# Second stack, layer 0: the context's norm and queries computed beside the end of the first stack

## The chip, the cores and the metric

The kernel runs on one core of one Trainium2 chip. The time is that of the device for one execution, in microseconds (us); the median of the runs counts.

## The reference

Two transformer stacks run one behind the other on x, 256 tokens of width 1024, all in float32.

The first stack has two layers. Each adds four branches to x, every one normed before and after: a gated feed-forward block (ffn0), a mixer, a second feed-forward block (ffn1) and a gated per-layer embedding (ple): `x = x + rmsnorm(sigmoid(h @ w_ple_gate) * (p @ w_ple_proj))`.

The second stack takes x and a context of another 256 tokens, which the first stack doesn't touch. Its layer 0 begins so:

```python
h  = modulate(rmsnorm(x,  norm1_g), sh1,  sc1)     # 256 tokens
hc = modulate(rmsnorm(xc, norm1_g), shc1, scc1)    # 256 context tokens
q, k, v    = split(h  @ w_qkv)                     # 1024 columns each; q and k are rotated by position
qc, kc, vc = split(hc @ w_qkv)                     # the context is not rotated
```

Attention over both, an output projection, a router and a mixture of 32 experts follow, then layer 1 of the same kind and a final norm. Shifts and scales (modulation) come from another input, by products with mod_w that are made piecewise beside the first stack.

## The kernel before

Each of the five engines has one program, a fixed list of instructions in order; an engine that waits holds back all that stands behind in its list. `pe_program`, `act_program`, `dve_program`, `pool_program` and `sp_program` write these lists for TensorE, ScalarE, VectorE, GpSimd and the queue that issues the loads. Semaphores carry the dependences: `s["name"].up(...)` is the signal, `s["name"].at(...)` the wait.

x and the context lie side by side in `k.x` (128 partitions, 8 tiles of the width, 512 columns: 256 tokens of x, then 256 of the context). `S` is 256, `KT` is 8, `D` is 1024. PSUM has 8 banks (`k.ps`) of 512 columns.

The end of the first stack (`pe_ple` and its companions, layer 1): the gate's quarters 0 and 1 are multiplied (L1281), the embedding projected (L1298), then quarters 2 and 3 (L1271), whose weights are the last loads of the stack (L1245). ScalarE makes the sigmoids (L1318), VectorE multiplies them with the projection (L1335). The post norm is a chain over four engines: squares (ScalarE L470), pair sums (VectorE L488, L491), the sum over partitions by a product with ones (TensorE L481), root (ScalarE L472), reciprocal (VectorE L493), and for each of the 8 tiles scale and add into x (VectorE L497, L500). The last of these is `added (1, "ple", 7)`.

The start of the second stack waits for that last add. Then ScalarE squares all 512 columns of each tile (L1376), TensorE sums them (L1369), ScalarE takes two roots (L1385), VectorE two reciprocals (L1403) and 16 scaled tiles (L1408), and ScalarE adds the shifts (L1390): 256 columns at a time, x and context in turn. SP issues the constants (L2973) and the six chunks of w_qkv, 2 MB each, into `slots2` (L1354), behind the same add.

`pe_project("q0")` makes 8 query tiles of 512 columns (x and context in one product, L1443), each followed by the rotation of the tile before it (L1425), for which ScalarE copies the x half (L1463); ScalarE also copies the context half (L1465), and VectorE finishes the rotation (L1477, L1479, L1482). `pe_project("k0")` does the same for the keys, `pe_values` makes the values (L1497), then comes attention. The experts' weights are issued at L1902, each behind a tile of TensorE that frees its slot.

A float32 product is recorded as two MATMUL and two LDWEIGHTS records.

Of the kernel before, what the change touches and what calls it, by code (L numbers as in the profile page):

```python
# [13 lines left out]
P = 128  # L14
D = 1024
# [18 lines left out]
class Signal:  # L34
# [27 lines left out]
    "pe_mod": "mod_product mod_turned", "pe_mixer": "mx_product mx_pe", "pe_ple": "ple_product ple_p_turned", "pe_tokens": "t_summed",  # L62
# [4 lines left out]
    "act_mixer": "mx_act", "act_ple": "ple_gated", "act_tokens": "t_squared t_root t_made", "act_project": "pr_copied", "act_values": "v_out_act",  # L67
# [9 lines left out]
    "pool_setup": "zeros_set upad_zero", "pool_squares": "squares conv_u", "pool_moe": "pool_ended", "pool_pairs": "xs_paired",  # L77
# [81 lines left out]
class Kernel:  # L159
# [99 lines left out]
    def second_memory(self):  # L259
        self.top = self.keep_top  # L260
        self.slots2 = [self.take(4096) for _ in range(6)]
        self.const2 = self.constants("constants_const2", second_constants(), 1850)
        self.h2 = self.take(KT, 2 * S)
        self.Q, self.K, self.V = (self.take(KT, 2 * S) for _ in range(3))
        self.pad = self.arena[:, self.top:self.top + 4096]
        self.sqb = self.take(4, BANK)
        self.take(KT * S - 4 * BANK)
# [9 lines left out]
        self.Kflat = self.K.rearrange("p a b -> p (a b)")  # L277
        self.vtok = [self.Vflat.rearrange("p (t d) -> p t d", t=4), self.Vflat[:, 0:1024].rearrange("p (t d) -> p t d", t=4)]
# [185 lines left out]
def act_post_norm(k, l, name, y, ready):  # L464

    act, s = k.nc.scalar, k.s
    act.activation(k.spare, k.eps, ACT.Sqrt)
    for b in range(4):
        act.wait_ge(*ready[b])
        act.activation(k.sq[:, 2 * b:2 * b + 2, :], y[:, 2 * b:2 * b + 2, :], ACT.Square).then_inc(*s["post_squared"].up(l, name, b))  # L470
    act.wait_ge(*s["post_summed"].at(l, name))
    act.activation(k.rscale[:, 0:S], k.ps[:, 0, 0:S], ACT.Sqrt, scale=1.0 / D, bias=k.eps[:, 0:1]).then_inc(*s["post_root"].up(l, name))  # L472
# [173 lines left out]
def pe_ffn(k, l, f):  # L646
# [61 lines left out]
    for c in range(2, CHUNKS):  # L708
        m = mods_of(l, f, c)
        gate_up(2 * c, k.h)  # L710
        down(2 * c - 1)
        gate_up(2 * c + 1, k.h)
        if m is not None:
            pe_modulate(k, l, m, m % 2, (2 * c + 2) % 4)
        down(2 * c)
        if m is not None:
            pe_modulation_out(k, l, m, (2 * c + 3) % 4, k.mrow, 0)
    down(2 * CHUNKS - 1)
# [30 lines left out]
def act_ffn(k, l, f):  # L749
# [25 lines left out]
    act_post_norm(k, l, f"ffn{f}", k.banks(4, 4, S), ends)  # L775

# [461 lines left out]
def sp_ple(k, l):  # L1238
# [17 lines left out]
    if l == 0:  # L1256
        sp_modulation(k, l, 10)
        sp_modulation(k, l, 11)
    sp.wait_ge(*s["ple_product"].at(l, "up", 3))
    quarter(3)  # L1260


def pe_ple(k, l):
# [40 lines left out]
    quarter(3, k.h)  # L1304
    pe_post_norm(k, l, "ple")


def act_ple(k, l):
    act, s = k.nc.scalar, k.s
    for b in range(4):  # L1310
        e = k.e[:, 2 * b:2 * b + 2, :]
        if b < 2:
            act.wait_ge(*s["ple_scaled"].at(l, b))
            src = e
        else:
            act.wait_ge(*s["ple_product"].at(l, "gate", b))
            src = k.banks(b, 1, S)
        act.activation(e, src, ACT.Sigmoid).then_inc(*s["ple_gated"].up(l, b))  # L1318
    act_post_norm(k, l, "ple", k.e, [s["ple_done"].at(l, b) for b in range(4)])


def dve_ple(k, l):
# [42 lines left out]
def pe_sums(k, tag, t, w):  # L1365

    pe, s = k.nc.tensor, k.s
    pe.wait_ge(*s["t_squared"].at(tag, t))
    pe.matmul(k.ps[:, 7, 0:w], k.c["ones"], k.sqb[:, t % 4, 0:w], start=(t == 0), stop=(t == KT - 1), skip_group_check=True).then_inc(*s["t_summed"].up(tag, t))  # L1369


def act_square(k, tag, t, w):
    act, s = k.nc.scalar, k.s
    if t >= 4:
        act.wait_ge(*s["t_summed"].at(tag, t - 4))
    act.activation(k.sqb[:, t % 4, 0:w], k.x[:, t, 0:w], ACT.Square).then_inc(*s["t_squared"].up(tag, t))  # L1376
# [37 lines left out]
def pe_project(k, tag, first, slots, ntok, tiles, dup=False, made=None, behind=None):  # L1414


    pe, s = k.nc.tensor, k.s
# [10 lines left out]
    for j in range(tiles):  # L1428
        slot = slots[j // 4]
        w = chunk_view(k, slot, n)  # L1430
        if j % 4 == 0:
            pe.wait_ge(*s[f"slot{slot}"].at("chunk", first + j // 4))
# [1529 lines left out]
def sp_program(k, ms, out):  # L2962
# [9 lines left out]
    sp.wait_ge(*s["zeroed"].at(1, D // 2))  # L2972
    sp.dma_start(*k.const2).then_inc(*s["const2"].up())  # L2973
    a = k.a
    w = a["a_w_qkv_2"][0]
    for n in range(6):
# [23 lines left out]
def pe_program(k, ms):  # L3000
    pe, s = k.nc.tensor, k.s
    pe_setup(k)
    for l in range(DEPTH):
# [33 lines left out]
def act_program(k, ms):  # L3037
# [39 lines left out]
def dve_program(k, ms):  # L3077
# [8 lines left out]
    V.wait_ge(*s["zeroed"].at(1, D // 2))  # L3086
    dve_modulated(k, "a0", 0, 0, (0, 1))
    V.wait_ge(*s["const2"].at())
    dve_project(k, "q0", k.Q, 2 * S, 8)
# [18 lines left out]
def pool_program(k, ms):  # L3108
# [3 lines left out]
    for l in range(DEPTH):  # L3112
# [3 lines left out]
        pool_prepare(k, l, "ffn1", added_before(k, l, "mix"))  # L3116
        pool_prepare(k, l, "ple", added_before(k, l, "ffn1"))
# [39 lines left out]
```

## Time and profile before

| | |
|---|---|
| median of 3 runs | 3017.91 us (3016.14 to 3020.22) |
| the profiled execution: its time, its span | 3016.83 us, 3015.6 us |
| busy: TensorE, VectorE, ScalarE, GpSimd | 2670.6, 751.3, 483.6, 212.8 us |
| last gate product of the ple block ends | 1396.58 us after the start |
| last add into x ends | 1413.25 us |
| first query product begins, first key product begins | 1429.08, 1489.76 us |

How to read the rows below. PE is TensorE's products, PEld its weight loads, DVE VectorE, ACT ScalarE, POOL GpSimd, SPq the load queue. L1443 is a line of the kernel. A row of the chain has the start, the length and what ran; the chain is followed back from the last instruction to whatever released it. A row of stretches has, for each engine in the order PE, PEld, DVE, ACT, POOL, the busy time and the instructions, then TensorE's granted clock (1.00 is 2.4 GHz, 0.50 is 1.2 GHz), the share of the DMA engines and GB/s. A row of a timeline has the start, the time from the first start to the last end of the merged instructions (for loads, of their issuing), the engine, line, operation, tiles and count, and in brackets the idle time before and what ended it. A row of groups has the count, then busy us, mean ns of one, idle us before them. A row of DMA issues has the count, the size and the us from issue to landing.

### The profile page before, as it was taken

What the parts mean: (1) busy time and instruction counts of PE and PEld (TensorE: products, weight loads), DVE (VectorE), ACT (ScalarE), POOL (GpSimd) and SP (SyncE); (2) the same over time, 40 slices, a digit from 0 to 9 for tenths busy, and PEclk for the clock granted to TensorE, in tenths of its full rate; (3) what the DMA queues carried; (4) which work ended last, traced back from release to release, by engine and by line L of the source; (5) the groups of instructions that cost most, each with busy time, mean ns of one, the idle gap of its engine ahead of it and who ended that gap; (6) DMA issues with size and microseconds to landing.
All of it is one profiled execution on the core that took longest, in us unless ns stands there. A gap on an engine that the chain in (4) does not pass through costs nothing.

```text
span 3015.6 us, 57462 instructions
## 1 busy us (share of the span) xinstructions
PE 2670.6 (89%) x24534; PEld 1982.5 (66%) x24534; DVE 751.3 (25%) x2039; ACT 483.6 (16%) x1182; POOL 212.8 (7%) x392
## 2 busy tenths in 40 slices
PE   8999999999999999997998899988776998776676
PEld 7888788887888778885444456665555466544444
DVE  2002520023002430014116621211113163332323
ACT  2001310011001220003104521110002151000001
POOL 1001010011001010001000012221211000000000
PEclk9999999999999999998999999999988999999999
DMA  7553465546453455542320039999996314999997
GB/s 265 179 171 112 157 239 173 174 157 223 153 192 111 162 202 203 195 157 106 144 84 29 3 144 375 411 411 421 420 420 236 105 52 179 420 419 419 419 419 296
DMA packets 251832, 690.23 MB, mean 229 GB/s; under 512 B 15247, under 2 KB 142942, under 8 KB 235230
## 3 DMA queue, kind: packets, MB, share of 16 engines
q1 hardware_dynamic: 240352, 675.27, 59.0%
q0 software_dynamic: 7552, 10.76, 1.0%
q8 instruction: 173, 2.83, 0.4%
q10 hardware_dynamic: 3710, 0.99, 0.1%
q14 instruction: 45, 0.37, 0.0%
HBM read 669.95 MB, written 17.04 MB: 228 GB/s over the span
## 4 chain that ended last, share of the span: by engine, by line
PE 76%; DMA 12%; DVE 5%; issue 3%; ACT 3%; SPq 0%; ACTq 0%; POOL 0%; POOLq 0%; DVEq 0%
PE ps L663 18%; DMA arena<-in_moe_w_up 11%; PE ps L674 10%; PE ps L1443 5%; PE ps L2287 5%; PE ps L2262 3%; PE ps L2790 3%; PE ps L2302 3%; PE ps L1497 2%; PE ps L894 2%; PE ps L687 2%; PE ps L1054 2%; PE ps L2042 2%; PE ps L2751 1%; PE ps L2814 1%
## 5 line engine op out<-in xcount | busy, mean ns | idle before, releaser
L663 PE MATMUL ps<-arena 128*128 128x256 f32 x2560 | 568.6, 379 | 3.5 <-DVE arena L745 3.5
L663 PEld LDWEIGHTS ps<-arena 128*128 128x128 f32 x2560 | 483.0, 189 | 73.8 <-issue 4.1
L674 PE MATMUL ps<-arena 128*128 128x256 f32 x1408 | 318.0, 379 | 0.0
L674 PEld LDWEIGHTS ps<-arena 128*128 128x128 f32 x1408 | 264.9, 189 | 46.1 <-issue 8.4
L2287 PE MATMUL ps<-arena 128*32 128x128 f32 x6016 | 193.6, 286 | 61.1 <-issue 58.6
L2287 PEld LDWEIGHTS ps<-arena 128*32 128x32 f32 x6016 | 177.6, 115 | 71.9 <-issue 67.6
L2790 PE MATMUL ps<-arena 128*32 128x128 f32 x4096 | 138.7, 294 | 82.3 <-issue 80.6
L787 DVE TENSOR_TENSOR arena<-arena,ps 128x256 f32<-128x256 f32 x76 | 32.1, 422 | 638.4 <-ACT arena L755 633.7
L2790 PEld LDWEIGHTS ps<-arena 128*32 128x32 f32 x4096 | 125.5, 118 | 90.0 <-issue 89.0
L1443 PE MATMUL ps<-arena 128*128 128x512 f32 (+1 forms) x384 | 162.6, 601 | 5.6 <-ACT arena L1390 5.6
L755 ACT ACTIVATE arena<-ps 128x256 f32<-128x256 f32 x76 | 29.2, 384 | 675.1 <-PE ps L663 675.1
L1443 PEld LDWEIGHTS ps<-arena 128*128 128x128 f32 (+1 forms) x384 | 64.6, 174 | 94.7 <-issue 91.7
L532 POOL TENSOR_TENSOR arena<-arena 128x256 f32<-128x256 f32 x64 | 42.8, 670 | 1081.3 <-DVE arena L500 1072.4
L2262 PE MATMUL ps<-arena 128*32 128x256 f32 x1536 | 103.1, 395 | 11.6 <-issue 8.5
L2369 POOL DMA_DIRECT2D expert_out<-arena x200 | 100.3, 502 | 69.8 <-issue 30.9
L2302 PE MATMUL ps<-arena 128*32 128x256 f32 x1504 | 94.3, 387 | 0.2
L2814 PE MATMUL ps<-arena 128*32 128x256 f32 x1024 | 62.1, 381 | 35.9 <-DVE arena L2902 35.9
L2347 DVE TENSOR_TENSOR arena<-arena,ps 128x128 f32<-128x128 f32 x47 | 13.5, 288 | 310.6 <-ACT arena L2317 310.6
L2262 PEld LDWEIGHTS ps<-arena 128*32 128x32 f32 x1536 | 57.4, 112 | 37.8 <-issue 14.0
L894 PE MATMUL ps<-arena 128*128 128x256 f32 x352 | 77.4, 379 | 0.0
L2751 PE MATMUL ps<-arena 128*32 128x256 f32 x528 | 69.8, 637 | 6.2 <-DVE arena L2006 3.3
L894 PEld LDWEIGHTS ps<-arena 128*128 128x128 f32 x352 | 66.3, 189 | 9.5
(457 smaller groups left out, 3091.6 us busy)
## 6 DMA issues: line engine op xcount, KB each, us to landing
arena<-in_moe_w_gate SPq DMA_DIRECT2D x64, 2048.0 KB, 24.8
arena<-in_moe_w_up SPq DMA_DIRECT2D x64, 2048.0 KB, 25.5
arena<-in_moe_w_down SPq DMA_DIRECT2D x64, 2048.0 KB, 30.4
arena<-in_mod_w SPq DMA_DIRECT2D x24, 2048.0 KB, 13.0
arena<-in_w_gate SPq DMA_DIRECT2D x44, 1024.0 KB, 5.3
arena<-in_w_up SPq DMA_DIRECT2D x44, 1024.0 KB, 7.9
arena<-in_w_down SPq DMA_DIRECT2D x44, 1024.0 KB, 4.8
arena<-in_w_in SPq DMA_DIRECT2D x12, 1024.0 KB, 6.0
```

The lines of the kernel that those rows point to most:

```text
L663: last = pe.matmul(k.ps[:, T % 4, off:off + S], w[:, t, T % 2 * P:(T % 2 + 1) * P], h[:, t, :], start=(t == 0), stop=(t == KT - 1), skip_g ...
L674: last = pe.matmul(acc[:, t, :], d[:, T % 2, t * P:(t + 1) * P], k.hid[:, T % 4, :], start=(T == 0 and t % 2 == 0), stop=end, skip_group_c ...
L687: last = pe.matmul(k.ps[:, T, off:off + S], w[:, t, T * P:(T + 1) * P], k.hu[:, t, :], start=(t == 0 and off == 0), stop=(t == KT - 1), sk ...
L894: last = pe.matmul(dst, w[:, t, j * P:(j + 1) * P], src[:, t, :], start=(t == 0), stop=(t == KT - 1), skip_group_check=True)
L1443: last = pe.matmul(k.ps[o:o + m, j % 4, 0:ntok], w[:, t, c0:c0 + m], k.h2[:, t, 0:ntok], start=(t == 0), stop=(t == KT - 1), tile_position ...
L2262: last = k.nc.tensor.matmul(k.ps[32 * q:32 * q + 32, 1, 0:256], m.pick[:, t, :], m.rows[:, t, 256 * q:256 * q + 256], start=(t == 0), stop ...
L2287: last = pe.matmul(ps[BL * q:BL * q + BL, 0, a:a + F], m.xeT[:, t, :], wv[:, t, F * q:F * q + F], start=(t == 0), stop=(t == KT - 1), tile ...
L2302: last = pe.matmul(ps[BL * q:BL * q + BL, 3, 0:W], m.hT[:, f, :], wd[:, f, W * q:W * q + W], start=(f == 0), stop=(f == 3), tile_position= ...
L2369: k.nc.gpsimd.dma_start(k.ybuf[bass.ds(b * BL, BL), W * q:W * q + W], m.yring[BL * q:BL * q + BL, bass.ds((b & 3) * W, W)]).then_inc(which ...
L2751: last = k.nc.tensor.matmul(k.ps[32 * q:32 * q + 32, bank, 0:256], m.pick[:, t, :], rows, start=(t == 0), stop=(t == 1), tile_position=(0, ...
L2790: last = pe.matmul(ps[BL * q:BL * q + BL, 0, a:a + F], m.xeT[:, t, :], wv[:, t, F * q:F * q + F], start=(t == 0), stop=(t == KT - 1), tile ...
L2814: last = pe.matmul(ps[BL * q:BL * q + BL, 3, 0:W], m.hT[:, f, :], wd[:, f, W * q:W * q + W], start=(f == 0), stop=(f == 3), tile_position= ...
```

## The change

Context and x are treated apart at the start of the second stack.

- GpSimd squares the context (8 tiles) and adds the squares up behind its ffn1 squares of layer 1, in the place of the later queries.
- TensorE sums them over partitions with one product ahead of the last down product of ffn1; ScalarE takes the root behind ffn1's post norm.
- VectorE's gain, reciprocal and 8 scaled context tiles stand in the ple block between the two `ple_scaled` and the gate multiplications; ScalarE's 8 shifts stand between the sigmoids 1 and 2.
- The query weights (two halves of 2 MB) go to the places of the keys and the values. Half 0 is issued once the modulation product 11 is done, half 1 right behind quarter 3 of the gate. The constants follow on quarter 2's product. Behind the last add SP issues only chunks 2 to 5.
- The context's 8 query tiles of 256 columns: 0 and 1 ahead of the ple block's post norm sums, 2 to 5 behind them, then the 8 sums of x, now over 256 columns, then tiles 6 and 7. ScalarE copies them to `k.Q` at the matching places.
- `pe_project("q0")` makes 8 tiles of 256 columns. x has its squares in 8 places of their own, so a square waits for no sum; each square waits for its own add instead of the last. The dummy root of L3053 goes.

```diff
 def act_post_norm(k, l, name, y, ready):
...
+    if (l, name) == (1, "ple"):
+        act_context_queries(k, (0, 1))
     act.wait_ge(*s["post_summed"].at(l, name))
...
 def pe_ffn(k, l, f):
...
+    if (l, f) == (1, 1):
+        pe_context_sum(k)
     down(2 * CHUNKS - 1)
     pe_post_norm(k, l, name)
...
 def act_ffn(k, l, f):
...
+    if (l, f) == (1, 1):
+        act_context_root(k)
...
 def sp_ple(k, l):
...
+    else:
+        sp.wait_ge(*s["mod_product"].at(l, 11))
+        sp_query_weights(k, 0)
     sp.wait_ge(*s["ple_product"].at(l, "up", 3))
     quarter(3)
+    if l == 1:
+        sp_query_weights(k, 1)
+        sp.wait_ge(*s["zeroed"].at(1, D // 2))
+        sp.wait_ge(*s["ple_product"].at(l, "gate", 2))
+        sp.dma_start(*k.const2).then_inc(*s["const2"].up())
...
+def sp_query_weights(k, i):
+    sp, s = k.nc.sync, k.s
+    sp.dma_start(k.qweights[i], columns(k.a["a_w_qkv_2"][0], 512 * i)).then_inc(*s[f"slot{i}"].up("chunk", i))
...
 def pe_ple(k, l):
...
     quarter(3, k.h)
+    if l == 1:
+        pe_context_queries(k, (0, 1))
     pe_post_norm(k, l, "ple")
...
 def act_ple(k, l):
...
         act.activation(e, src, ACT.Sigmoid).then_inc(*s["ple_gated"].up(l, b))
+        if (l, b) == (1, 1):
+            act_context_shifts(k)
...
 def dve_ple(k, l):
...
+    if l == 1:
+        dve_modulated(k, "a0", 0, 0, (1,))
     for b in range(4):
...
+CONTEXT_BANKS = (1, 2, 3, 4, 5, 6, 1, 2)
+
+def pool_context_squares(k):
+    pool, s = k.nc.gpsimd, k.s
+    pool.wait_ge(*s["added"].at(1, "mix", KT - 1))
+    for t in range(KT):
+        pool.tensor_tensor(k.csq[:, t, :], k.x[:, t, S:2 * S], k.x[:, t, S:2 * S], ALU.mult).then_inc(*s["c_squares"].up(t))
+        if t > 0:
+            pool.wait_ge(*s["c_squares"].last())
+            pool.tensor_tensor(k.csq[:, 0, :], k.csq[:, 0, :], k.csq[:, t, :], ALU.add).then_inc(*s["c_squares"].up(t, "added"))
+
+def pe_context_sum(k):
+    pe, s = k.nc.tensor, k.s
+    pe.wait_ge(*s["c_squares"].at(KT - 1, "added"))
+    pe.matmul(k.ps[:, 0, S:2 * S], k.c["ones"], k.csq[:, 0, :], start=True, stop=True, skip_group_check=True).then_inc(*s["c_summed"].up())
+
+def act_context_root(k):
+    act, s = k.nc.scalar, k.s
+    act.wait_ge(*s["zeroed"].at(1, D // 2))
+    act.wait_ge(*s["c_summed"].at())
+    act.activation(k.at[:, 0, S:2 * S], k.ps[:, 0, S:2 * S], ACT.Sqrt, scale=1.0 / D, bias=k.eps[:, 0:1]).then_inc(*s["t_root"].up("a0", 1))
+
+def act_context_shifts(k):
+    act, s = k.nc.scalar, k.s
+    for t in range(KT):
+        H = k.h2[:, t, S:2 * S]
+        act.wait_ge(*s["t_normed"].at("a0", t, 1))
+        act.activation(H, H, ACT.Identity, bias=k.mod_col(0, 0, t, 1)).then_inc(*s["t_made"].up("a0", t, 1))
+
+def pe_context_queries(k, tiles):
+    pe, s = k.nc.tensor, k.s
+    free = [s["ple_scaled"].at(1, 1), s["ple_gated"].at(1, 2), s["ple_gated"].at(1, 3), s["ple_done"].at(1, 0), s["ple_done"].at(1, 1), s["ple_done"].at(1, 2),
+            s["c_out"].at(0), s["c_out"].at(1)]
+    for j in tiles:
+        if j % 4 == 0:
+            pe.wait_ge(*s[f"slot{j // 4}"].at("chunk", j // 4))
+        if j == 0:
+            pe.wait_ge(*s["t_made"].at("a0", KT - 1, 1))
+        pe.wait_ge(*free[j])
+        for t in range(KT):
+            last = pe.matmul(k.ps[:, CONTEXT_BANKS[j], 0:S], k.qweights[j // 4][:, t, j % 4 * P:(j % 4 + 1) * P], k.h2[:, t, S:2 * S],
+                             start=(t == 0), stop=(t == KT - 1), skip_group_check=True)
+        last.then_inc(*s["c_tile"].up(j))
+
+def act_context_queries(k, tiles):
+    act, s = k.nc.scalar, k.s
+    for j in tiles:
+        act.wait_ge(*s["c_tile"].at(j))
+        act.activation(k.Q[:, j, S:2 * S], k.ps[:, CONTEXT_BANKS[j], 0:S], ACT.Copy).then_inc(*s["c_out"].up(j))
...
 def pe_project(k, tag, first, slots, ntok, tiles, dup=False, made=None, behind=None):
...
+        w = chunk_view(k, slots[j // 4], n) if slots else k.qweights[j // 4]
+        if not slots and j == 1:
+            pe.wait_ge(*s["c_out"].at(7))
...
 def pe_program(k, ms):
...
+    pe_context_queries(k, (2, 3, 4, 5))
     for t in range(KT):
-        pe_sums(k, "a0", t, 2 * S)
+        pe_sums(k, "a0", t)
+    pe_context_queries(k, (6, 7))
     pe.wait_ge(*s["const2"].at())
-    pe_project(k, "q0", 0, (0, 1), 2 * S, 8, made=[s["t_made"].at("a0", t, 1) for t in range(KT)])
+    pe_project(k, "q0", 0, None, S, 8, made=[s["t_made"].at("a0", t, 0) for t in range(KT)])
...
 def act_program(k, ms):
...
-    act.wait_ge(*s["added"].at(1, "ple", KT - 1))
-    act.wait_ge(*s["zeroed"].at(1, D // 2))
-    act.activation(k.lnA[:, 0, KT:KT + 1], k.eps, ACT.Sqrt)
     for t in range(KT):
-        act_square(k, "a0", t, 2 * S)
-    act_modulated(k, "a0", 0, 0, (0, 1))
-    act_project(k, "q0", k.Q, 2 * S, 8)
+        act.wait_ge(*s["added"].at(1, "ple", t))
+        act_square(k, "a0", t)
+    act_context_queries(k, (2, 3, 4, 5))
+    act_modulated(k, "a0", 0, 0, (0,))
+    act_context_queries(k, (6, 7))
+    act_project(k, "q0", k.Q, S, 8)
```

## Rows read from the trace of the kernel before

**Rows 1.** The page: the chain that ended last, by engine.

```profile
PE 76%; DMA 12%; DVE 5%; issue 3%; ACT 3%; SPq 0%; ACTq 0%; POOL 0%; POOLq 0%; DVEq 0%
```

**Rows 2.** Stretches from the last gate quarters to the end of the queries.

```profile
1382.70:1396.60 13.90, 13.87 (x64) 11.76 (x63) 0.69 (x1) 0.60 (x1) 0.00 (x0) 1.00 0.23 77
1396.60:1404.90 8.30, 3.50 (x8) 2.28 (x8) 2.08 (x3) 4.19 (x8) 0.00 (x0) 0.80 0.00 0
1404.90:1413.25 8.35, 0.00 (x0) 0.00 (x0) 7.79 (x17) 0.45 (x1) 0.00 (x0) 0.70 0.00 0
1413.25:1429.10 15.85, 9.47 (x17) 3.92 (x17) 5.20 (x9) 6.71 (x14) 0.00 (x0) 0.72 0.95 354
1429.10:1489.76 60.66, 60.62 (x145) 27.99 (x146) 12.98 (x34) 10.69 (x30) 0.00 (x0) 0.97 0.45 166
```

**Rows 3.** The chain that ended last, in order of time, 1099 to 1503.

```profile
1099.27 1.83 PE ps L481 x8
...
1382.70 13.88 PE ps L1271 x64
...
1401.33 3.51 PE ps L481 x8
...
1414.04 9.46 PE ps L1369 x16
...
1424.10 3.38 DVE arena L1403 x2
...
1429.08 15.63 PE ps L1443 x32
...
1452.02 0.43 PE ps L1425 x2
...
1489.06 0.70 PE ps L1425 x2
1489.76 13.76 PE ps L1443 x32
```

**Rows 4.** Groups of instructions, shapes apart, 1370 to 1489.8.

```profile
L1271 PEld LDWEIGHTS ps<-arena 128*128 128x128 f32 x64 | 12.1, 189 | 1.8
...
L1408 DVE SCALAR_TENSOR_TENSOR arena<-arena 128x256 f32<-128x256 f32 x16 | 6.4, 482 | 0.0
```

**Rows 5.** Timeline of the ple block: loads issued, ScalarE and VectorE.

```profile
1350.42 32.69 SPq L1245 DMA_DIRECT2D arena<-in_w_ple_gate  x2
...
1356.10 0.51 ACT L519 ACTIVATE arena<-arena 128x256 f32<-128x256 f32 x1 [3.07 <-DVE arena L500]
...
1376.45 1.28 DVE L1330 TENSOR_TENSOR arena<-ps,arena 128x512 f32<-128x512 f32 x2
...
1389.67 0.60 ACT L1318 ACTIVATE arena<-ps 128x512 f32<-128x512 f32 x1 [11.27 <-PE ps L1271]
```

**Rows 6.** VectorE's add beside GpSimd (min/median/max ns); timeline of ffn1's start.

```profile
L500 DVE TENSOR_TENSOR arena<-arena x8: 417/606/718, 1355.6 to 1361.5; 128x256 f32<-128x256 f32 x8
...
1114.43 1.53 POOL L535 TENSOR_TENSOR arena<-arena 128x256 f32<-128x256 f32 x2
...
1122.16 2.36 DVE L579 TENSOR_TENSOR arena<-arena 128x1024 f32<-128x1024 f32 x2
...
1125.56 0.43 DVE L787 TENSOR_TENSOR arena<-arena 128x256 f32<-128x256 f32 x1 [0.22 <-ACT arena L755]
...
1128.38 7.07 PE L674 MATMUL ps<-arena 128*128 128x256 f32 x32
```

**Rows 7.** DMA issues: quarter 3, a pair of 1184, the six chunks.

```profile
arena<-in_w_ple_gate SPq DMA_DIRECT2D x1, 1024.0 KB, 4.8
...
arena<-in_w_gate SPq DMA_DIRECT2D x1, 1024.0 KB, 5.3
arena<-in_w_up SPq DMA_DIRECT2D x1, 1024.0 KB, 7.9
...
arena<-in_a_w_qkv SPq DMA_DIRECT2D x6, 2048.0 KB, 19.7
```

More of the change, by code:

```diff
@@ L61 @@
     "pe_setup": "setup_turned cols_turned", "pe_norm": "post_summed norm_summed", "pe_gate_up": "ffn_gu", "pe_down": "ffn_down",
-    "pe_mod": "mod_product mod_turned", "pe_mixer": "mx_product mx_pe", "pe_ple": "ple_product ple_p_turned", "pe_tokens": "t_summed",
+    "pe_mod": "mod_product mod_turned", "pe_mixer": "mx_product mx_pe", "pe_ple": "ple_product ple_p_turned", "pe_tokens": "t_summed c_summed c_tile",
     "pe_project": "pr_tile pr_rot", "pe_values": "v_tile", "pe_attend": "sc_done tw_turned av_done", "pe_out": "o_turned out_tile",
@@ L66 @@
     "act_setup": "setup_out_act rope_sin cs_ready lam_exp", "act_norm": "post_squared post_root made norm_root", "act_ffn": "ffn_silu mod_row",
-    "act_mixer": "mx_act", "act_ple": "ple_gated", "act_tokens": "t_squared t_root t_made", "act_project": "pr_copied", "act_values": "v_out_act",
+    "act_mixer": "mx_act", "act_ple": "ple_gated", "act_tokens": "t_squared t_root t_made c_out", "act_project": "pr_copied", "act_values": "v_out_act",
     "act_attend": "sc_exp wt_act tw_act av_squared av_out_act", "act_out": "o_root o_out", "act_router": "r_act r_rows_out",
@@ L75 @@
     "dve_moe": "moe_combined moe_added", "dve_rows": "xr_step", "dve_picked": "xs_step", "dve_final": "final_step",
-    "pool_setup": "zeros_set upad_zero", "pool_squares": "squares conv_u", "pool_moe": "pool_ended", "pool_pairs": "xs_paired",
+    "pool_setup": "zeros_set upad_zero", "pool_squares": "squares conv_u c_squares", "pool_moe": "pool_ended", "pool_pairs": "xs_paired",
 }
@@ L266, in second_memory @@
         self.sqb = self.take(4, BANK)
+        self.xsq = self.sqb.rearrange("p a b -> p (a b)").rearrange("p (a b) -> p a b", a=KT)
         self.take(KT * S - 4 * BANK)
@@ L277, in second_memory @@
         self.Kflat = self.K.rearrange("p a b -> p (a b)")
+        self.csq = self.Qflat[:, 0:KT * S].rearrange("p (a b) -> p a b", a=KT)
+        self.qweights = [t.rearrange("p (k f) -> p k f", k=KT) for t in (self.Kflat, self.Vflat)]
         self.vtok = [self.Vflat.rearrange("p (t d) -> p t d", t=4), self.Vflat[:, 0:1024].rearrange("p (t d) -> p t d", t=4)]
@@ L1362, in columns, with pe_sums, act_square @@
     return w.rearrange("(k p) f -> p k f", p=P)[:, :, at:at + n]
-def pe_sums(k, tag, t, w):
+def pe_sums(k, tag, t):
     pe, s = k.nc.tensor, k.s
     pe.wait_ge(*s["t_squared"].at(tag, t))
-    pe.matmul(k.ps[:, 7, 0:w], k.c["ones"], k.sqb[:, t % 4, 0:w], start=(t == 0), stop=(t == KT - 1), skip_group_check=True).then_inc(*s["t_summed"].up(tag, t))
-def act_square(k, tag, t, w):
+    pe.matmul(k.ps[:, 7, 0:S], k.c["ones"], k.xsq[:, t, :], start=(t == 0), stop=(t == KT - 1), skip_group_check=True).then_inc(*s["t_summed"].up(tag, t))
+def act_square(k, tag, t):
     act, s = k.nc.scalar, k.s
-    if t >= 4:
-        act.wait_ge(*s["t_summed"].at(tag, t - 4))
-    act.activation(k.sqb[:, t % 4, 0:w], k.x[:, t, 0:w], ACT.Square).then_inc(*s["t_squared"].up(tag, t))
+    act.activation(k.xsq[:, t, :], k.X1[:, t, :], ACT.Square).then_inc(*s["t_squared"].up(tag, t))
 def act_modulated(k, tag, which, l, streams):
@@ L1428, in pe_project @@
     for j in range(tiles):
[L1429 to L1432, printed above, removed]
+        w = chunk_view(k, slots[j // 4], n) if slots else k.qweights[j // 4]
+        if slots and j % 4 == 0:
+            pe.wait_ge(*s[f"slot{slots[j // 4]}"].at("chunk", first + j // 4))
+        if not slots and j == 1:
+            pe.wait_ge(*s["c_out"].at(7))
         if j >= 4:
@@ L2971, in sp_program @@
     sp.wait_ge(*s["added"].at(1, "ple", KT - 1))
-    sp.wait_ge(*s["zeroed"].at(1, D // 2))
-    sp.dma_start(*k.const2).then_inc(*s["const2"].up())
     a = k.a
     w = a["a_w_qkv_2"][0]
-    for n in range(6):
+    for n in range(2, 6):
         sp_chunk(k, n, n, columns(w, 512 * n))
@@ L3085, in dve_program @@
     V.wait_ge(*s["added"].last())
-    V.wait_ge(*s["zeroed"].at(1, D // 2))
-    dve_modulated(k, "a0", 0, 0, (0, 1))
+    dve_modulated(k, "a0", 0, 0, (0,))
     V.wait_ge(*s["const2"].at())
-    dve_project(k, "q0", k.Q, 2 * S, 8)
+    dve_project(k, "q0", k.Q, S, 8)
     dve_project(k, "k0", k.K, 2 * S, 8)
@@ L3116, in pool_program @@
         pool_prepare(k, l, "ffn1", added_before(k, l, "mix"))
+        if l == 1:
+            pool_context_squares(k)
         pool_prepare(k, l, "ple", added_before(k, l, "ffn1"))
```

## The prediction

> **What bounds the kernel now.** I read the page's chain first: TensorE carries three quarters of what ended last [rows 1], so a stretch in which it stands idle is the place where time can be taken. Then I cut the end of the first stack and the start of the second into stretches [rows 2]. The reader is to see that TensorE is full up to 1396.60 and again from 1429.10, and that between them lie 8.30, 8.35 and 15.85 us in which it is busy 3.50, 0.00 and 9.47 us. The granted clock falls there to 0.80, 0.70 and 0.72; it is 1.00 in the dense stretches, so that the work which does stand in the gap runs partly at the lower level of 1.2 GHz. The chain in order of time [rows 3] names that work: the post norm's sums take 3.51 us (1.83 in the mixer's post norm, where TensorE comes straight from its products), the second stack's sums over 512 columns 9.46, both reciprocals together 3.38, and the first two query tiles 15.63 against 13.76 for the first two key tiles at the full clock. From the end of the gate's last quarter (1396.58) to the first key product (1489.76) the chain runs 93.18 us. Nothing in this stretch waits for a transfer, and in the code the loads further on wait only for tiles of TensorE behind this point, so a shift of the key products carries on to the end.
>
> **What the change moves on TensorE.** A 512 column tile is 16 records in 6.88 us (two key tiles in 13.76 [rows 3]). It becomes two tiles of 256 columns. The gate quarters are the same shape, 128x128 weights by 256 columns, and 64 of them run in 13.88 us [rows 3], 0.217 each; a narrow tile is 16 x 0.217 = 3.47 us. I take that price for all 16 narrow tiles, so the split itself costs nothing and the eight context tiles are 27.7 us of work that can stand elsewhere. New order from 1396.58, all at the full clock since TensorE no longer rests:
> - context tiles 0 and 1: 6.94, to 1403.5. The post norm's sums could begin at 1401.33 [rows 3], so these two tiles push it by 2.2.
> - post norm sums: 1.83 instead of 3.51, to 1405.4. That is 0.5 later than the 1404.85 of before. The rest of that chain (root, reciprocal, scale and add) keeps its length, so the last sum into x comes at about 1413.8 instead of 1413.25.
> - context tiles 2 to 5: 13.9, to 1419.2. They cover the 8.4 us of VectorE work on which the engine stood idle, and the squares.
> - eight sums of 256 columns: 16 records x 0.217 = 3.5, to 1422.7. ScalarE makes each square as its x tile appears, so the last one is ready by 1414.3 and no sum waits.
> - context tiles 6 and 7: 6.9, to 1429.6. Beside them run root 0.48, one reciprocal 1.7 to 1.8 (half of 3.38 and the latency), the eight scaled tiles and the shifts. VectorE needs 6.4 us for 16 scaled tiles [rows 4] and ScalarE follows each with its shift, so eight take 3.3 with what lies between; the last shift is there at 1422.7 + 0.5 + 1.8 + 3.3 + 0.5 = 1428.8, 0.8 us ahead of need, and the last is needed only at the end of the first tile, 3 us further.
> - the query tiles of x: 8 x 3.47 = 27.7, and the rotations as before: six at 0.43 between the tiles and 1.17 at the end (0.43, 0.04, 0.70) [rows 3], together 31.5, to 1461.1.
>
> The sum is 27.7 + 1.8 + 3.5 + 31.5 = 64.5 us against 93.18, a gain of 28.7. VectorE and ScalarE follow in the query loop: three operations of VectorE on 256 columns, like the fastest add into x at 417 ns [rows 6], and one copy of ScalarE for a tile of 3.9 us on TensorE.
>
> **What it adds earlier.** One product of 256 columns (the context's sum) before the last down product of the second layer's ffn1: 2 x 0.217 = 0.43 us on the path, no cover. It leaves 28.2.
>
> The context's root on ScalarE, 0.48 us, stands behind the post norm's root and ahead of the first copy at 1356.10, before which ScalarE is idle for 3.07 us, waiting for VectorE [rows 5]; hidden. If that cover went, it would cost 0.5.
>
> VectorE's part (gain 0.2, reciprocal 1.75, eight scaled tiles 3.3) is 5.2 us put after the second ple_scaled, which ends at 1377.7. It pushes the first two gate multiplications to 1384.4. Both are wanted only at the post norm; the third waits for a sigmoid that starts at 1389.67 [rows 5], so the cover is over 5 us. ScalarE's eight shifts run beside them and end by 1384, in its 11.27 us of idle time before that sigmoid. Whether Identity needs a table load beside Sigmoid no row shows; from below nothing, from above two loads of 1.28 us, both inside that idle time. I take nothing. Context tile 0, at 1396.6, finds them done 12 us before.
>
> GpSimd's 15 squares and adds, about 0.7 us each, follow the ffn1 squares, which end at 1116 [rows 6], and run to about 1127. The sum that needs them is 200 us later. They run beside VectorE's start of ffn1, and there is a price in the trace: the add into x takes 606 ns in the median beside GpSimd's squares, 417 at least [rows 6]. At that ratio the two h products grow from 2.36 to 3.4 and the first hidden product comes at 1127.3 instead of 1126.0. TensorE wants it at 1128.4, so 1.1 us of cover is left. From below nothing, from above (all 5.6 us of VectorE's work there at that ratio) 0.1 to 0.6; I take nothing.
>
> **SP's queue and the transfers.** Half 0 of the query weights is issued when the last modulation product is done, before the gate's first products and so before 1357; it is wanted 40 us later. It stands ahead of quarter 3 in the queue, but its wait ends 26 us before quarter 3's. Quarter 3 is issued at 1383.1 (1350.42 + 32.69) and lands in 4.8 [rows 7], 1387.9, for products that start at 1389.6: a cover of 1.7 us. Half 1 now follows right behind it on the same queue. The nearest row is a gate weight chased by an up weight of the same size: 5.3 for the first, 7.9 for the second, so the first loses at most 0.5; I take nothing for quarter 3. From above, if both shared the engines evenly, quarter 3 would take 4.8 + 2.6 = 7.4 and cost 0.8. Half 1 is wanted by tile 4 at 1412; six such loads and the constants in one queue landed in 19.7 in the median [rows 7], and this one has a single megabyte ahead of it, 29 us of cover. The constants move to 1390. The four chunks left for keys and values are issued at 1413.8; even 20 us later they are there at 1434, for keys that now start at 1461.
>
> **Weight loads under narrow products.** The gap of the narrow product is the number on which all hangs. The weight load takes 189 ns and hides inside 217 in the gate's quarters [rows 3, 4]; a product of 256 columns takes 0.43 us there, one of 512 columns 0.86. The Trainium skill (TensorE: Matmul & The Clock Gate, Back-to-back issue gap) gives a sustained stream about 81 ns at 128 columns and 131 at 512, so that cost does not halve with the columns. As an estimate from that page, 98 at 256 would make two halves 1.5 times the whole, 27 us dearer on 55, and the gain would shrink to about 1. The trace disagrees with it for these products, and the sum goes by the trace.
>
> **Rivals.**
> A, the sum above: 28.2 us less. The likeliest, 0.80.
> B, a cover fails in part: quarter 3 late by 0.8, VectorE slowed beside GpSimd, the post norm's chain late behind the context copies on ScalarE, or the clock not full in one of the pieces (a us at 1.2 GHz costs half a us of work). Each is worth 0.5 to 4, together 6 at most by the rows: 22 to 27 less, 2991 to 2996. For it speaks the thin cover of 1 to 2 us in three places; against it that each miss is small. 0.12.
> C, the gain is not passed on: some load of the expert stage starts by its own time and ends last, as the chain's 12% of transfers suggest [rows 1]. Every one of those loads waits for a tile of TensorE behind the key products, so it would move along. If half were lost, 14 less, 3004. 0.03.
> D, on the other side: the narrow products show their weight load. There are 16 narrow tiles x 16 = 256 records; each ns of load that is not hidden costs 0.256 us. It decides at 28.2 / 256 = 110 ns: with the whole 189 open the cost is 48.4 and the kernel is 20 slower, 3038. For it speaks that the load already fills 189 of 217 ns; against it that 64 gate records in a row pay none of it. By the rule of the Trainium skill above it would stop just short of the turn, at no change. Slower 0.03, no change 0.02.
>
> **How the numbers follow.** The profiled execution took 3016.83 us (span 3015.6), 1.1 below the median of the runs shown, 3017.91. 3016.83 - 28.2 = 2988.6 for a like execution, and 3017.91 - 28.2 = 2989.7 for the median, which I predict. The range goes up to 2997 for B, and down to 2985: a further 2 if the runs spread as before (4 us from lowest to highest), and 2 to 3 if later stages meet a better clock. A alone is 2986 to 2992. A measurement tells 0.2%, 6 us, from no change; faster is A, B and C, 0.95, the same 0.02, slower 0.03.
>
> **What would show it.** In the changed profile: TensorE busy over 95% from 1396 to the first key product at a clock of 1.00; context tiles at 3.47 us; post norm sums below 2.1; the first key product at about 1461.5 (1461.1 and the 0.43). Wrong if a narrow tile takes over 4 us, if quarter 3 or the first context tile waits, or if the gap before the first query tile of x is more than a us.

## The result

The changed kernel takes 2992.65 us in the median of 4 runs (2989.69 to 2993.97), the kernel before 3017.86 (3016.14 to 3020.22). The ratio is 0.9915, with a 95% interval from 0.9897 to 0.9932: faster by 25.2 us. A later series of 5 runs against 15 of the kernel before gave 0.9908 (0.9895 to 0.9922). The prediction was 2989.7 with a range from 2985 to 2997.

The stretches of the profile after, cut at the same events as [rows 2] (end of the up projection, end of the gate, end of the post norm's sums, end of context tiles 6 and 7, first key product; columns as there):

```profile
1381.97:1395.84 13.87, 13.87 (x65) 12.11 (x65) 2.06 (x4) 1.34 (x3) 0.00 (x0) 1.00 0.82 296
1395.84:1404.48 8.64, 8.64 (x41) 7.55 (x41) 2.08 (x3) 4.82 (x9) 0.00 (x0) 1.00 0.00 0
1404.48:1428.70 24.22, 24.22 (x114) 21.16 (x113) 12.97 (x27) 9.18 (x23) 0.00 (x0) 1.00 0.63 227
1428.70:1460.14 31.44, 31.40 (x145) 27.13 (x145) 8.14 (x21) 3.46 (x9) 0.00 (x0) 1.00 0.45 161
```

TensorE's busy time equals the length of each stretch to 0.04 us, and the granted clock is 1.00 in all four. In [rows 2] it was busy 3.50 of 8.30, none of 8.35 and 9.47 of 15.85 us, at clocks of 0.80, 0.70 and 0.72.

The chain that ended last, to be laid beside [rows 3] (L1294 the gate's quarters 2 and 3, L1416 context tiles, L486 the post norm's sums, L1458 x's sums, L1532 query and key tiles, L1513 rotations):

```profile
1381.97 13.87 PE ps L1294 x64
1395.84 6.92 PE ps L1416 x32
1402.75 1.73 PE ps L486 x8
1404.48 13.84 PE ps L1416 x64
1418.32 3.47 PE ps L1458 x16
1421.78 6.92 PE ps L1416 x32
1428.70 6.92 PE ps L1532 x32
1435.62 0.43 PE ps L1513 x2
...
1459.43 0.70 PE ps L1513 x2
1460.14 13.76 PE ps L1532 x32
```

Where [rows 3] hand the chain from TensorE to ScalarE and VectorE and back, it stays here on one engine; the only row of "issue" between the gate and the first key product is one of 0.04 us ahead of the last rotation. From the end of the gate to the first key product it takes 1460.14 - 1395.84 = 64.30 us against 93.18, which is 28.9 less. The gate ends 0.7 us earlier too, so the first key product comes 29.6 us earlier. Yet the spans of the two first profiles differ by 25.0 us only (3015.6 and 2990.6). The experiments had to say where the other 4.6 us went.

### The profile page after: what moved, and what is told of

Read it like the earlier page. It is cut to its first block, busy times and chain, and to the rows that moved or that the text cites. A ratio compares the mean times of both kernels' runs of the same rounds, so it can differ in the third digit from the quotient of the medians.

```text
span 2990.6 us, 57737 instructions
## 1 busy us (share of the span) xinstructions
PE 2663.9 (89%) x24664; PEld 2009.8 (67%) x24664; DVE 752.3 (25%) x2039; ACT 482.7 (16%) x1181; POOL 224.3 (7%) x407
## 4 chain that ended last, share of the span: by engine, by line
PE 76%; DMA 13%; DVE 5%; ACT 3%; issue 3%; SPq 0%; ACTq 0%; POOL 0%; POOLq 0%; DVEq 0%
PE ps L668 19%; DMA arena<-in_moe_w_up 12%; PE ps L679 10%; PE ps L2376 5%; PE ps L1532 4%; PE ps L2879 3%; PE ps L2351 2%; PE ps L1586 2%; PE ps L2391 2%; PE ps L903 2%; PE ps L692 2%; PE ps L1063 2%; PE ps L2131 2%; PE ps L2840 1%; PE ps L2903 1%
## 5 line engine op out<-in xcount | busy, mean ns | idle before, releaser
L1532 PE MATMUL ps<-arena 128*128 128x256 f32 (+2 forms) x384 | 134.1, 527 | 0.0
L2351 PE MATMUL ps<-arena 128*32 128x256 f32 x1536 | 103.1, 397 | 10.6 <-issue 7.5
L1532 PEld LDWEIGHTS ps<-arena 128*128 128x128 f32 (+1 forms) x384 | 64.1, 172 | 63.1 <-issue 58.6
```

Of the source, the lines that this page charges most:

```text
L1532: last = pe.matmul(k.ps[o:o + m, j % 4, 0:ntok], w[:, t, c0:c0 + m], k.h2[:, t, 0:ntok], start=(t == 0), stop=(t == KT - 1), tile_position ...
L2351: last = k.nc.tensor.matmul(k.ps[32 * q:32 * q + 32, 1, 0:256], m.pick[:, t, :], m.rows[:, t, 256 * q:256 * q + 256], start=(t == 0), stop ...
```

## The experiments

Where a profile is compared below, one measure serves for all: from the start of the last gate record to the start of the first value record ("gate to values"), and from there to the end of the span ("tail"). The first holds every edit below except the wait of half_ahead, and the keys; the second is the same code in all kernels. The 0.43 us that the change adds ahead of the gate lie in neither. The figures come from rows such as these, the value products of the changed kernel and of the kernel before (min/median/max ns, then first and last start; L1586 and L1497 are the same line of the code):

```profile
L1586 PE MATMUL ps<-arena x192: 377/590/596, 1518.8 to 2393.7; 128*128 128x512 f32 x128, 128*128 128x256 f32 x64
```

```profile
L1497 PE MATMUL ps<-arena x192: 377/590/595, 1548.4 to 2419.4; 128*128 128x512 f32 x128, 128*128 128x256 f32 x64
```

| run | last gate record | first value | gate to values | tail | ratio to before (95%) |
|---|---|---|---|---|---|
| before, first profile | 1396.2 | 1548.4 | 152.2 | 1467.2 | |
| again_before | 1394.8 | 1547.0 | 152.2 | 1475.3 | |
| after, first profile | 1395.5 | 1518.8 | 123.3 | 1471.8 | 0.9915 (0.9897 to 0.9932) |
| again_after | 1396.6 | 1519.9 | 123.3 | 1472.7 | 0.9908 (0.9895 to 0.9922) |
| split_in_place | 1397.1 | 1551.0 | 153.9 | 1470.4 | 1.0004 (0.9994 to 1.0014) |
| kept_warm | 1391.5 | 1538.3 | 146.8 | 1472.2 | 0.9976 (0.9965 to 0.9987) |
| two_tiles_later | 1392.3 | 1522.7 | 130.4 | 1469.3 | 0.9931 (0.9911 to 0.9950) |
| all_tiles_behind | 1397.0 | 1534.3 | 137.3 | 1468.2 | 0.9953 (0.9936 to 0.9969) |
| half_ahead | 1401.5 | 1524.9 | 123.4 | 1469.4 | 0.9935 (0.9919 to 0.9952) |
| one_sum | 1395.3 | 1515.6 | 120.3 | 1468.5 | 0.9888 (0.9871 to 0.9904) |
| one_sum_both | 1396.9 | 1515.9 | 119.0 | 1469.6 | 0.9889 (0.9874 to 0.9904) |
| one_sum_both_2 | 1395.3 | 1514.3 | 119.0 | 1469.4 | 0.9901 (0.9885 to 0.9918) |

Gate to values repeats to 0.1 us wherever a kernel ran twice. Its neighbours do not: what stands before the last gate record moves by 1.1 to 1.6 us between two profiles of one kernel, and by 5.6 over the four kernels that share the old code there (4.7 over the seven with the new code, half_ahead left out), and the tail moves by up to 8.

**again_after and again_before: both kernels once more.** No edit; again_before is a single execution of 3023.53 us, near the top of the kernel's range (3014.51 to 3023.59).

> The changed kernel once more, unchanged. In its first profile the key products began 29.6 us earlier than before, but the span ended only 25.0 us earlier: from the first key product to the end it took 1530.5 us, before 1525.8. Theory A (chance: the stages of many small products behind the keys, where the granted clock changes between its two levels dozens of times, vary from execution to execution): this profile's time from the first key product to the end lies anywhere between 1525 and 1531, while everything up to the first key product repeats within 0.5 us. Theory B (the change lengthens what stands behind it): 1530 to 1531 again. The ratio to before should be 0.990 to 0.992 under both.

> The kernel before once more, for a second profile. Theory A (chance in the stages behind the keys): up to the first key product within 0.5 us of the 1489.8 of the first profile, and from there to the end 1525 to 1531. Theory B (the change lengthens what stands behind the keys): from the first key product to the end 1525 to 1526.5 again.

The gain between gate and values is 28.9 us in both pairs of profiles. From the first key product to the end the changed kernel took 1530.5 and 1531.4 us, the kernel before 1525.8 and then 1534.0. In the table's measure the second tail of the kernel before is 8.1 longer than its first and longer than any other. So theory B, which had 1525 to 1526.5 for the kernel before, falls: the tail is not longer because of the change. Theory A was too narrow as well. It had 1525 to 1531 for both kernels, and the first key product repeated only to 1.1 and 1.4 us, where 0.5 was expected; and again_after taken alone, 1531.4, could not tell A from B. The first profile of the kernel before happened to have the shortest tail of the twelve. The four kernels that have the old order up to the keys show 1467.2 to 1475.3, mean 1471.3; the eight with the new order 1468.2 to 1472.7, mean 1469.9.

One stage of the tail shows a part of this scatter. This is the attention of layer 0, first score product to first turned tile, in five profiles: before, again_before, after, again_after, two_tiles_later.

```profile
1604.40:1705.00 100.60, 74.66 (x416) 47.76 (x416) 79.55 (x195) 64.35 (x227) 0.00 (x0) 0.90 0.06 22
```

```profile
1603.00:1703.60 100.60, 74.64 (x417) 47.73 (x417) 79.58 (x195) 64.34 (x227) 0.00 (x0) 0.90 0.06 22
```

```profile
1574.80:1677.30 102.50, 75.55 (x417) 48.52 (x417) 79.72 (x195) 64.44 (x227) 0.00 (x0) 0.90 0.06 21
```

```profile
1575.90:1675.50 99.60, 72.91 (x416) 46.35 (x416) 79.33 (x195) 64.22 (x227) 0.00 (x0) 0.93 0.06 22
```

```profile
1578.70:1676.00 97.30, 70.12 (x416) 44.60 (x416) 79.39 (x195) 64.16 (x227) 0.00 (x0) 0.96 0.06 22
```

The instructions are the same. VectorE and ScalarE are busy for the same 79.5 and 64.3 us; TensorE, busy between 70 and 76 us, is what differs, with the mean granted clock: 97.3 us at 0.96, 99.6 at 0.93, 100.6 and 102.5 at 0.90. In attention TensorE stops for each step of the softmax, and its mean clock differs from execution to execution.

But this stage does not explain the tails. The two profiles of the kernel before have the same 100.60 us here and tails 8.1 us apart. From the first to the last value record, which takes in the experts of layer 0, they take 871.0 and 874.1 us; the other 5.0 arise behind. For the whole execution time and clock go together: of 35 executions of the kernel before, the 12 with a mean granted clock of 0.959 or less took 3021.8 us on average, the 8 with 0.962 or more 3017.4. That the clock causes all of the scatter is not shown.

**split_in_place: the split alone.** In the kernel before, each query tile in two series of products:

```diff
+            for a, b in ((0, S), (S, 2 * S)) if tag == "q0" else ((0, ntok),):
             for t in range(KT):
...
-                last = pe.matmul(k.ps[o:o + m, j % 4, 0:ntok], w[:, t, c0:c0 + m], k.h2[:, t, 0:ntok], ...
+                last = pe.matmul(k.ps[o:o + m, j % 4, a:b], w[:, t, c0:c0 + m], k.h2[:, t, a:b], ...
```

> The kernel before, where each of the eight 512 column query tiles is made as two products series of 256 columns in the same place. Nothing is moved. Theory A (a narrow tile costs half of a wide one, weight loads stay hidden): the queries take 0.1 us more in all, and as the first tile's first half needs only the shifts of x and the context in turn, the first tile may end within 1 us of before; the time stays within 0.1%. Rival (narrow products show their weight load of 189 ns, in part or in whole): 256 records of 256 columns, up to 48 us more, and 24 more if half of it is open.

Gate to values grew by 1.7 us, and the ratio is 1.0004. The chain of this kernel (L1390 the shifts, L1444 the query products):

```profile
1429.46 6.50 ACT arena L1390 x16
...
1436.01 11.07 PE ps L1444 x50
```

A later tile is 32 records in 6.91 us in the same chain, against 6.88 for 16 wide ones: 0.2 us for all eight, where 0.1 was expected. The other 1.5 are at the first tile. Its x half cannot end before the last of the 16 shifts, and only then does the context half begin; a wide product takes both in the same pass. I had said at most 1. That loss is not in the changed kernel, where the shifts of x come alone and while TensorE is busy. The rival of an open weight load is refuted: 256 narrow records cost 0.2 us, not 24 or 48.

**kept_warm: the clock alone.** In the kernel before, TensorE's rest is filled with products that nobody reads:

```diff
+def pe_fill(k, n):
+    for i in range(n):
+        k.nc.tensor.matmul(k.ps[:, 1, 0:S], k.c["ones"], k.x[:, i % KT, S:2 * S], start=True, stop=True, skip_group_check=True)
...
     quarter(3, k.h)
+    if l == 1:
+        pe.wait_ge(*s["ple_scaled"].at(1, 1))
+        pe_fill(k, 10)
     pe_post_norm(k, l, "ple")
+    if l == 1:
+        pe_fill(k, 22)
...
     for t in range(KT):
         pe_sums(k, "a0", t, 2 * S)
+    pe_fill(k, 12)
```

> The kernel before with products that nobody reads in TensorE's idle time: 10 of 256 columns ahead of the ple block's post norm sums, 22 behind them, 12 behind the second stack's sums (0.43 us each), so that the clock stays up. It separates the two parts of the gain: rest filled with useful work, and work that stands in the gap at the lower clock. Theory A (the clock part is 1.7 on the post norm, 2.5 on the sums and 1.9 on the first two query tiles): the key products begin 5 to 6.5 us earlier than before and the time is 0.15 to 0.2% less. Rival (the chain over the four engines sets the time and TensorE's pace in it does not matter): within 1.5 us of before.

5.4 us less from gate to values, inside the 5 to 6.5 expected, and a ratio of 0.9976 (7 us less, the interval reaches from 4 to 11; 0.15 to 0.2%, 4.5 to 6 us, was expected). The post norm's sums took 2.00 us, x's wide sums 6.89 instead of 9.46, the first two query tiles 14.00 instead of 15.63:

```profile
1396.61 2.00 PE ps L481 x8
1398.61 9.50 PE ps L1372 x44
1408.11 6.89 PE ps L1379 x16
...
1420.57 14.00 PE ps L1453 x32
```

The granted clock (the third figure from the right) was 1.00 over the whole gap:

```profile
1391.86:1398.61 6.75, 6.30 (x29) 5.19 (x29) 2.08 (x3) 4.17 (x7) 0.00 (x0) 1.00 0.00 0
1398.61:1408.11 9.50, 9.50 (x46) 8.25 (x45) 8.03 (x19) 1.54 (x4) 0.00 (x0) 1.00 0.04 6
1408.11:1420.57 12.46, 12.06 (x40) 7.23 (x40) 4.94 (x6) 5.51 (x12) 0.00 (x0) 1.00 0.99 372
```

About a fifth of the gain is thus clock: the few products that must stand in the gap run at 2.4 GHz throughout, where the kernel before had mean clocks of 0.80, 0.70 and 0.72. The rest can be added up from rows. TensorE's idle time between the gate and the first query tile was 4.80 + 8.35 + 6.38 = 19.5 us in [rows 2], and the changed kernel has none. Its sums over x are 3.47 us instead of the 6.89 that wide ones take at the full clock, because GpSimd has added up the context's squares: 3.4 more. With the 5.4 that is 28.3 of the 28.9 us.

**two_tiles_later and all_tiles_behind: where the cover stands.** In the changed kernel, context tiles 0 and 1 behind the post norm's sums; in the second, all eight behind x's sums.

```diff
     quarter(3, k.h)
-    if l == 1:
-        pe_context_queries(k, (0, 1))
     pe_post_norm(k, l, "ple")
...
-    pe_context_queries(k, (2, 3, 4, 5))
+    pe_context_queries(k, (0, 1, 2, 3, 4, 5))
```

```diff
     quarter(3, k.h)
-    if l == 1:
-        pe_context_queries(k, (0, 1))
     pe_post_norm(k, l, "ple")
...
-    pe_context_queries(k, (2, 3, 4, 5))
     for t in range(KT):
         pe_sums(k, "a0", t)
-    pe_context_queries(k, (6, 7))
+    pe_context_queries(k, range(8))
```

> The changed kernel with context tiles 0 and 1 behind the post norm's sums of the ple block instead of ahead of them (six tiles stand behind them). Theory A (what counts is that TensorE never rests; the push of 2.2 us on the post norm is cheaper than the rest it fills): TensorE is idle 4.75 us ahead of the sums again, the granted clock falls, the sums take 3.5 instead of 1.7 and part of what follows runs at the lower level; the key products begin 6.5 to 8.5 us later than in the changed kernel, 0.2 to 0.3% slower than it. Rival (the norm's chain sets the time, and tiles ahead of it push it): within 1 us of the changed kernel, or faster by up to 2.

> The changed kernel with all eight context tiles behind x's eight sums, so that they cover only the root, the reciprocal and the first scaled tiles. Theory A (the gain is TensorE's rest filled with work, and its full clock): TensorE rests 4.75 us ahead of the post norm and some 8 us behind it, the sums follow the adds one by one, and the key products begin 13 to 15 us later than in the changed kernel; the time is 0.45 to 0.5% above it and still 0.35 to 0.45% under before. Rival (the gain comes from work taken off the chain behind the last add, half the squares, sums, reciprocals and scaled tiles, wherever the tiles stand): within 4 us of the changed kernel.

Gate to values: 130.4 and 137.3 us, 7.1 and 14.0 above the changed kernel; the ratios are 0.9931 and 0.9953. Both distances lie inside what theory A gave. Timeline of TensorE in two_tiles_later and then in all_tiles_behind (idle time before a row in brackets):

```profile
1397.47 3.78 PE L484 MATMUL ps<-arena 128*128 128x256 f32 x8 [4.77 <-DVE arena L494]
```

```profile
1402.18 3.65 PE L484 MATMUL ps<-arena 128*128 128x256 f32 x8 [4.77 <-DVE arena L494]
1409.88 6.62 PE L1454 MATMUL ps<-arena 128*128 128x256 f32 x16 [4.06 <-ACT arena L1459]
```

The 4.77 us of rest are back in both, and the sums take 3.8 and 3.7 us instead of 1.7. Pushing the post norm by two tiles costs its chain 0.4 us (its sums end at 1404.48; the pair sums end at 1400.56, and 3.5 us of cold sums behind them would have ended at 1404.1) and costs the end nothing, since TensorE has other work until the chain returns. In all_tiles_behind a second rest, 4.06 us, stands ahead of x's sums (some 8 was expected), and these take 6.62 us instead of 3.47, since they follow the adds one by one at a lower clock.

The rival of all_tiles_behind was that the gain comes from the shorter chain of x alone, wherever the tiles stand, to within 4 us. It falls, since 14.0 us are lost. But 14.9 of the 28.9 us remain, so the shorter chain is a real part while TensorE still waits for it. x's sums end 19.1 us after the gate (1397.43 to 1416.50), before 26.9 (1396.58 to 1423.50): 7.9 us less. The other 7.0 come behind the sums, where the tiles cover the 5.6 us for which the first query tile waited before. In the changed kernel the chain is covered completely, and what counts is TensorE's work alone.

**half_ahead: the cover of quarter 3.**

```diff
+    if l == 1:
+        sp_query_weights(k, 1)
     quarter(3)
     if l == 1:
-        sp_query_weights(k, 1)
```

> The changed kernel with half 1 of the query weights issued ahead of the gate's quarter 3 instead of behind it. It tests how much cover quarter 3's transfer has. Theory A (one queue, in order: 2 MB ahead of it take 5.4 us more, against a cover of 1.7): quarter 3 lands 10 to 11 us after the issue, the products that need it start 3 to 4 us late, the key products begin that much later, and the time is 0.1 to 0.13% above the changed kernel. Rival (two transfers in flight share, or the transfer is covered anyway): under 1 us.

Quarter 3 landed after 10.6 us instead of 5.2, with half 1 ahead of it. The issues of quarter 3 in the changed kernel and in half_ahead:

```profile
arena<-in_w_ple_gate SPq DMA_DIRECT2D x1, 1024.0 KB, 5.2
```

```profile
arena<-in_w_ple_gate SPq DMA_DIRECT2D x1, 1024.0 KB, 10.6
```

TensorE waited 4.15 us, just above the 3 to 4 expected. But then the products behind the wait ran partly at the lower clock (0.81 in the mean over their 8.9 us), which I had not counted. Chain, and timeline of TensorE, of half_ahead:

```profile
1382.41 10.59 DMA arena<-in_w_ple_gate
1392.99 0.04 issue
1393.04 8.88 PE ps L1295 x32
```

```profile
1393.04 8.88 PE L1295 MATMUL ps<-arena 128*128 128x256 f32 x32 [4.15 <-DMA arena<-in_w_ple_gate]
```

8.88 us for work of 6.94: a wait of 4.15 us cost 4.15 + 1.95 = 6.1. The ratio is 0.9935, 8 us above again_after's (6 above the first series'), where 0.1 to 0.13% (3 to 4 us) was expected: too little by about half. The local 6.1 account for most of it; the rest is within the intervals.

**one_sum, one_sum_both, one_sum_both_2: less work for TensorE.** VectorE adds x's squares, TensorE sums once; in the second also in the ple block's post norm.

```diff
+def dve_add_squares(k, tag):
+    for t in range(1, KT):
+        V.wait_ge(*s["t_squared"].at(tag, t))
...
+        V.tensor_tensor(k.xsq[:, 0, :], k.xsq[:, 0, :], k.xsq[:, t, :], ALU.add)...
...
 def pe_program(k, ms):
-    for t in range(KT):
-        pe_sums(k, "a0", t)
+    pe_one_sum(k, "a0")
...
 def dve_post_norm(k, l, name, y, gain):
+    if (l, name) == (1, "ple"):
...
+        V.tensor_tensor(k.sq[:, 0:2, :], k.sq[:, 0:2, :], k.sq[:, 6:8, :], ALU.add)...
+        V.tensor_tensor(k.sq[:, 0, :], k.sq[:, 0, :], k.sq[:, 1, :], ALU.add)...
```

> The changed kernel with fewer products by ones: VectorE adds x's eight squares as they come, and TensorE sums with one product instead of eight (saves 7 x 0.433 = 3.0 us of TensorE); in the ple block VectorE also adds the last pair and the two halves, so the post norm has one product instead of four (saves 1.3). Theory A (from the last gate quarter to the values TensorE is full, so each of its us is a us of the end as long as VectorE's chain stays ahead): the key products begin 4.3 us earlier than in the changed kernel, ratio to before 0.9895 to 0.990. Rival (the norm's chain, made longer by VectorE's adds, is what ends last): the first query product of x waits and the gain is under 1 us.

> Half of the step of one_sum_both: only x's squares are added by VectorE (one product by ones instead of eight, 3.0 us of TensorE less); the ple block's post norm keeps its four products. Theory A (every us of TensorE between the gate and the values is a us of the end): from the last gate product to the first value product it takes 120.3 us, between the changed kernel's 123.3 and the 119.0 of one_sum_both; ratio to before about 0.9898. Rival (one of the two savings gave nothing): 119.0 or 122.0.

> The version with fewer sums on both places once more, to narrow its interval: last gate product to first value product 119.0 us again, ratio to before 0.9885 to 0.9900.

120.3 and twice 119.0 us from gate to values, 3.0 and 4.3 below the changed kernel, as worked out. The seven adds of VectorE end before TensorE comes to the sum (timeline of one_sum_both, L1482 the adds, L1473 the sum):

```profile
1413.11 3.61 DVE L1482 TENSOR_TENSOR arena<-arena 128x256 f32<-128x256 f32 x7
...
1418.35 0.59 PE L1473 MATMUL ps<-arena 128*128 128x256 f32 x2
```

The medians of one_sum, one_sum_both and one_sum_both_2 are 2985.03, 2986.36 and 2987.95 us, against 2992.65 and 2993.83 for the changed kernel. The total times do not put them in the order of the profiles: the kernel with one saving has the lowest median, and all three ratios miss what was expected, by 0.001 or less. The intervals of the ratios still touch those of the changed kernel; that these are the fastest kernels here, and that the second saving adds 1.3 us, rests on the profiles, where the step of 4.3 us came twice.

## Why the prediction was right, and where its 3 us went

- **The terms between gate and keys.** Predicted 64.5 us against 93.18, measured 64.30. Context tiles 27.7 (measured 27.68), post norm sums 1.8 (1.73), x's sums 3.5 (3.47), queries 31.5 (31.44). That a narrow tile costs half of a wide one was the step on which all hung; it is 3.46 us, and split_in_place shows it apart: two narrow tiles cost 0.03 us more than a wide one. The Trainium skill's sustained figures for narrow and wide products (TensorE: Matmul & The Clock Gate, Back-to-back issue gap), from which the prediction estimated that two halves would cost half as much again, do not hold for these float32 products.
- **The cover of the chain.** Predicted: the shifts of x done 0.8 us ahead of the first product. The last shift ended at 1428.01, the product began at 1428.54 without a wait. It holds, with half a us of cover (timeline after, L1477 the shifts):

```profile
1424.71 3.30 ACT L1477 ACTIVATE arena<-arena 128x256 f32<-128x256 f32 x8 [2.41 <-DVE arena L1495]
...
1428.54 7.08 PE L1532 MATMUL ps<-arena 128*128 128x256 f32 x32
```

- **The added product.** 0.43 us ahead of the last down product, on the path, as predicted:

```profile
1341.88 3.45 PE ps L679 x16
1345.34 0.43 PE ps L1387 x2
1345.77 2.60 PE ps L679 x12
```

- **GpSimd beside VectorE.** Predicted for the two h products 3.4 us instead of 2.36. They took 3.18, and the first hidden product ended 1.5 us before TensorE's first down product began, where 1.1 was predicted. The instructions with an operand in PSUM did not grow (L806: 0.41 and 0.42). Timeline of ffn1's start after, to lay beside [rows 6]:

```profile
1121.00 3.18 DVE L584 TENSOR_TENSOR arena<-arena 128x1024 f32<-128x1024 f32 x2
1121.51 1.59 POOL L1381 TENSOR_TENSOR arena<-arena 128x256 f32<-128x256 f32 x1
1123.06 1.59 POOL L1378 TENSOR_TENSOR arena<-arena 128x256 f32<-128x256 f32 x1
...
1124.25 0.41 DVE L806 TENSOR_TENSOR arena<-ps,arena 128x256 f32<-128x256 f32 x1
...
1125.21 0.53 DVE L796 TENSOR_TENSOR arena<-arena 128x256 f32<-128x256 f32 x1 [0.22 <-ACT arena L762]
...
1127.22 2.10 PE L679 MATMUL ps<-arena 128*128 128x256 f32 x9
```

- **The context's norm in the ple block.** Predicted end of the shifts by 1384, found 1382.71. There is no table load between Sigmoid and the shifts.

```profile
1376.43 1.23 ACT L1343 ACTIVATE arena<-arena 128x512 f32<-128x512 f32 x2 [3.66 <-DVE arena L1357]
...
1379.41 3.30 ACT L1402 ACTIVATE arena<-arena 128x256 f32<-128x256 f32 x8 [1.75 <-DVE arena L1495]
```

- **The transfers.** Quarter 3 landed in 5.2 us, 0.4 more than in [rows 7], the 0.5 that the pair of gate and up weights had given; TensorE did not wait. Half 1 landed after 10.2. (The upper bound for quarter 3, 2.6 us more against a cover of 1.7, comes to 0.9 and not 0.8.)
- **Rivals.** By the time alone A and B could not be told apart: the medians of both series, 2992.65 and 2993.83, lie in B's 2991 to 2996 and just outside A's 2986 to 2992. The profiles decide. No cover failed and the clock was 1.00 throughout, so B did not occur; between gate and values the gain is 28.9 - 0.43 = 28.5 us, where A had 28.2. C, half of the gain lost behind the keys, is refuted by the tails, which did not grow (means of 1469.9 and 1471.3). D is refuted by split_in_place.
- **What was off.** The step "3017.91 - 28.2 for the median" took the median of three runs as firm and let the runs spread by 4 us. Fifteen runs of the kernel before spread from 3014.51 to 3023.59, 9 us, with medians from 3017.86 to 3020.56 in the four series; its tail alone spread by 8 in two profiles. Against the 15 runs the gain is 26.7 us in medians and 27.8 by the ratio, 28.2 is well inside the interval. No term of the sum is off by 3 us, so I read the missing 3 us of the first series as the scatter of the rest of the kernel. That this accounts for all of the difference is argued from the twelve tails, not shown; a lasting loss of 1 us or so behind the keys could not be seen under them, and what makes the tails scatter is shown for one stage only.

## What to carry to other kernels

When one engine is the bound and a chain over other engines interrupts it, count the rest at its full price: the idle time, here 19.5 us, and the work around it at the lower clock, here 5.4 us or a fifth of the gain. Independent work fills such a rest even if it pushes the chain, as long as there is more of it behind; two tiles ahead of the norm were worth 7 us. Look also at what can be taken off the chain itself: while TensorE still waited for it, that was worth 7.9 us. Once the engine is full, look for what it need not do at all: sums by products went to an idle VectorE for 4.3 us. And measure such a step between two fixed events of the profile, where it repeats to 0.1 us, before reading it from total times that scatter by 9.

## What the runs showed of the hardware that was not expected

- The same attention of layer 0 took 97.3 to 102.5 us in five profiles, the shorter times at the higher mean granted clocks (0.96 to 0.90), with the other engines' busy times unchanged. The Trainium skill (TensorE: Matmul & The Clock Gate, Part 1: The HAM clock gate) has the clock at half rate after idle time and at full rate after sustained work; this case's rows agree: 1.00 in the four stretches of the changed kernel where TensorE is always busy, 0.70 to 0.80 in the gap of [rows 2], and 0.81 behind a single wait of 4.15 us, which cost 6.1.
- VectorE's two float32 products of 1024 columns, with both operands in the on-chip memory outside PSUM, took 3.18 instead of 2.36 us beside GpSimd, and the two GpSimd instructions beside them 1.59 us each instead of 0.73 and 0.61. VectorE's instructions with one operand in PSUM stayed at 0.41 to 0.43 us beside GpSimd.
